# Recurrent mixer's diagonal in its last level, value transposition after the decay transposition, masks ahead of the scores, compression input evicted in one piece

## What is computed

```python
# compression: segments of 16 tokens, 31 overlapping blocks of 32
flat = blocks.transpose(0, 1, 3, 2, 4).reshape(B, ncmp, G, CMP_LEN * dh)
return jax.nn.gelu(flat @ w1) @ w2
...
# recurrence, inside a chunk of 64 tokens: every pair s <= t, with its decay
decay = jnp.exp(jnp.where(causal[:, :, None], b[:, :, :, None, :] - b[:, :, None, :, :], -jnp.inf))
attn = jnp.einsum('bhtd,bhsd,bhtsd->bhts', qc, kc, decay)
...
# attention: scores of a query block, masked
s = jnp.einsum('bhmqd,bhmkd->bhmqk', qblk, kh).astype(jnp.float32) * scale
p = jax.nn.softmax(jnp.where(allowed, s, neg), axis=-1)
```

## Time and profile before

| | |
|---|---|
| three runs | 1952.78, 1953.26, 1955.55 us |
| median | 1953.26 us |
| the profiled execution, its own time | 1954.02 us |
| its span in the trace | 1952.2 us |
| mean granted clock of TensorE in it | 0.999 |
| PE busy | 98% of the span |
| VectorE, ScalarE, GpSimd busy | 47%, 43%, 45% |

### The profile page before, as it was taken

How to read it: one execution, slowest core, us unless ns; L and a number is a source line. 1 busy time by engine, 2 the same in 40 slices (tenths; PEclk the granted TensorE clock), 3 DMA queues, 4 the chain that set the end, 5 groups by cost and what they waited for, 6 DMA issues and landing times. The chain is left out here.

```text
span 1952.2 us, 25554 instructions
## 1 busy us (share of the span) xinstructions
PE 1919.8 (98%) x9142; PEld 1506.3 (77%) x9142; DVE 915.8 (47%) x1423; ACT 834.1 (43%) x1269; POOL 881.5 (45%) x1185
## 2 busy tenths in 40 slices
PE   8999999999999999999999999999999999999998
PEld 7766666888888887777688888887777688888887
DVE  6587877432231346777541313233777643222132
ACT  4456565543342355555532223134555543222233
POOL 4322211556456465343456456454443255454553
PEclk9999999999999999999999999999999999999999
DMA  8211111233233233222133233333222233243322
GB/s 229 65 44 44 33 44 33 87 108 108 87 91 115 77 96 98 76 66 76 55 104 113 81 104 100 85 98 96 76 67 75 65 87 110 85 119 86 109 86 76
DMA packets 318099, 168.50 MB, mean 86 GB/s; under 512 B 15027, under 2 KB 313494, under 8 KB 317846
## 3 DMA queue, kind: packets, MB, share of 16 engines
q1 hardware_dynamic: 314432, 162.38, 29.0%
q10 hardware_dynamic: 3542, 4.50, 0.9%
HBM read 160.29 MB, written 2.10 MB: 83 GB/s over the span
## 5 line engine op out<-in xcount | busy, mean ns | idle before, releaser
L744 POOL TENSOR_TENSOR wlo<-raw,whi 128x256 fp32r<-128x256 f32 x1160 | 864.4, 778 | 1039.5 <-ACT whi L791 1039.5
L1641 PE MATMUL accs<-Xh,whi 128*128 128x512 f32 x1448 | 581.2, 401 | 1.8 <-POOL wlo L744 1.8
L1642 PE MATMUL accs<-Xl,whi 128*128 128x512 f32 x1448 | 563.9, 389 | 0.0
L1644 PE MATMUL accs<-Xh,wlo 128*128 128x512 f32 x1440 | 562.0, 390 | 0.0
L791 ACT ACTIVATE whi<-raw 128x1024 fp32r<-128x1024 f32 x291 | 307.7, 1061 | 267.1 <-PE accs L1644 218.7
L1641 PEld LDWEIGHTS accs<-Xh,whi 128*128 128x128 f32 x1448 | 272.0, 188 | 60.1 <-POOL wlo L744 3.9
L1642 PEld LDWEIGHTS accs<-Xl,whi 128*128 128x128 f32 x1448 | 272.3, 188 | 56.3 <-issue 3.6
L1644 PEld LDWEIGHTS accs<-Xh,wlo 128*128 128x128 f32 x1440 | 270.3, 188 | 58.2
L1641 PE MATMUL accs<-Uh,whi 128*128 128x512 f32 x744 | 289.7, 389 | 0.8 <-DVE xT L1222 0.8
L1642 PE MATMUL accs<-Ul,whi 128*128 128x512 f32 x744 | 289.5, 389 | 0.0
L1644 PE MATMUL accs<-Uh,wlo 128*128 128x512 f32 x744 | 289.4, 389 | 0.0
(11 more groups left out here) (305 smaller groups left out, 1910.9 us busy)
## 6 DMA issues: line engine op xcount, KB each, us to landing
raw<-in_w_ff_dram SPq DMA_DIRECT2D x128, 512.0 KB
raw<-in_w_in_dram SPq DMA_DIRECT2D x71, 512.0 KB
raw<-in_w_gate_up_dram SPq DMA_DIRECT2D x44, 512.0 KB
raw<-in_w_down_dram SPq DMA_DIRECT2D x16, 512.0 KB
raw<-in_w_o_dram SPq DMA_DIRECT2D x16, 512.0 KB
px<-W ACTq DMA_DIRECT2D x64, 64.0 KB, 2.0
raw<-in_w_down_dram SPq DMA_DIRECT2D x8, 384.0 KB
W<-in_x_dram SPq DMA_DIRECT2D x4, 512.0 KB, 6.1
```

The lines of the kernel that those rows point to most:

```text
L744: pool.tensor_tensor(lo[:, ks], raw[:, unit_no % RAW, ks], hi[:, ks].bitcast(F32), ALU.subtract).then_inc(sems["wlo"], 1)
L1641: mmul(y, whi[:, slot, k], xh[:, k], start=(i == 0), stop=False)
L1642: last = mmul(y, whi[:, slot, k], xl[:, k], start=False, stop=("both" in u and i == len(ks) - 1))
L1644: last = mmul(y, wlo[:, slot, k], xh[:, k], start=False, stop=(i == len(ks) - 1))
```

## The change

It has five parts.

1. `hd` is gone. The mask of the last level has ones on its diagonal too. In that level (`m == 1`) the decays are made for 256 elements instead of 512, VectorE multiplies the odd key positions by exp(-d) and the odd query positions by exp(d) in place, in two instructions of 256 elements each, and PE multiplies keys and queries themselves: on the diagonal the factors cancel. `hP` of level 0 initialises `HA` by a product with its mask.
2. In `ORDER`, `vt2` comes behind `cb` and `ha2` for heads 0 to 2. In `LAST1` only `hd` is dropped.
3. In `n1`, `s1` and `d1` the mask matmuls come first and open the sum; the scores are added to them.
4. In `n1`, `s1` and `d1` the wait for the query or key (`nq_ok`, `sbk_ok`, `rope_ok`) stands behind the masks.
5. `evc` takes the unit out in one product of 128x512 into `q4`, which frees the bank. Two VectorE copies and two new ScalarE copies (64x256 each, strided) then make what the four products made.

```diff
+    lev[:, -1] += np.eye(P)
...
-    ("mmA", 0, "hg"), ("vt", 0), ("hd", 0), ("vt2", 0, "hv"), ("cb", 0), ("ha2", 0), ("n1", 0, 0, 2), ("mmB", 0, "hg"), ("hD", 0, 0),
+    ("mmA", 0, "hg"), ("vt", 0), ("cb", 0), ("ha2", 0), ("vt2", 0, "hv"), ("n1", 0, 0, 2), ("mmB", 0, "hg"), ("hD", 0, 0),
...
# ScalarE, evc
+                    act.wait_ge(sems["acc"], at("acc", 1))
+                    for g, odd in ((0, 1), (1, 0)):
+                        r = hrows(g)
+                        A(kcx[n][r].rearrange("p (h s) -> p h s", s=32), every2(t[r], odd), ACT.Copy).then_inc(sems["cmp_t" if g else "act"], 1)
# VectorE, evc
-                    for g, odd in ((0, 1), (1, 0)):
-                        r = hrows(g)
-                        TTn(kcx[n][r].rearrange("p (h s) -> p h s", s=32), every2(y[r], odd), every2(rstd[r], odd), ALU.mult).then_inc(sems["cmp_t" if g else "dve"], 1)
+                    t = q4[:, 3 - n]
+                    scaled(t, 1 - n)
                     for g, odd in ((0, 0), (1, 1)):
-                        TTn(kc2[n][r, g].rearrange("p (h s) -> p h s", s=32), every2(y[r], odd), every2(rstd[r], odd), ALU.mult).then_inc(sems["acc" if g else "dve"], 1)
+                        CP(kc2[n][r, g].rearrange("p (h s) -> p h s", s=32), every2(t[r], odd)).then_inc(sems["cmp_e" if g else "dve"], 1)
# VectorE, hd (removed) and hF of the last level
-                    TTn(HA, TT[:, 0, :].rearrange("p (b n) -> p b n", n=P), ident.unsqueeze(1).to_broadcast([P, NB, P]), ALU.mult).then_inc(sems["T_dve"], 1)
+                    if m == 1:
+                        k1, q1 = odds(hk[i % 2]), odds(hq[i % 2])
+                        TTn(k1, k1, HD[:, a % 2, T // 2:T], ALU.mult).then_inc(sems["dve"], 1)
+                        dve.wait_ge(sems["dve"], chained())
+                        TTn(q1, q1, HD[:, a % 2, 0:T // 2], ALU.mult).then_inc(sems["hl_f"], 1)
# VectorE, hP
+                    if a == 0:
+                        TTn(HA, F2, mask.bitcast(F32).unsqueeze(1).to_broadcast([P, NB, P]), ALU.mult).then_inc(sems["T_dve"], 1)
# PE, hd (removed)
-                    for b in range(NB):
-                        r = slice(P * b, P * b + P)
-                        last = mmul(TT[:, 0, r], hk[p][:, r], hq[p][:, r], start=True, stop=True)
# PE, n1 (s1 and d1 in the same way)
-                    pe.wait_ge(sems["nq_ok"], at(f"q{i}"))
                     pe.wait_ge(sems["S_act"], at("S_act"))
                     pe.wait_ge(sems["S_dve"], at("S_dve"))
                     for g in range(2):
-                        mmul(S[:, g, 0:n], q4[hrows(g), i % 2, P * qb:n], kts[a][hrows(g), 0:n], start=True, stop=False)
+                        mmul(S[:, g, n - P:n], identb, m_causal, start=True, stop=False, skip_group_check=True)
+                    pe.wait_ge(sems["nq_ok"], at(f"q{i}"))
                     for g in range(2):
-                        last = mmul(S[:, g, n - P:n], identb, m_causal, start=False, stop=True)
+                        last = mmul(S[:, g, 0:n], q4[hrows(g), i % 2, P * qb:n], kts[a][hrows(g), 0:n], start=False, stop=True, skip_group_check=True)
```

More of the change, by code:

```diff
@@ L101 @@
     "resid": dict(acc=1),
-    "evc": dict(acc=1, cmp_t=1),
+    "evc": dict(acc=1, cmp_t=1, cmp_e=1),
     "cmp1": dict(M_fill=1, M_dve=1, g_in=1, g_e=1, g_ok=1),
@@ L160, in marks_of @@
         return dict(xt_ok="acc")
-    if kind == "evc":
-        return {f"evc{item[1]}": "acc"}
     if kind == "mixo":
@@ L631, in hrows, with odds @@
             return slice(64 * g, 64 * g + 64)
+        def odds(v):
+            return v.rearrange("p (n t) -> p t n", t=2)[:, 1]
         def every2(v, odd):
@@ L1436, in stage @@
                     dve.wait_ge(sems["T_fill"], at(f"hF{a}"))
-                    dve.copy_predicated(HA, mask.unsqueeze(1).to_broadcast([P, NB, P]),
-                                            TT[:, a % 2, :].rearrange("p (b n) -> p b n", n=P)).then_inc(sems["T_dve"], 1)
+                    F2 = TT[:, a % 2, :].rearrange("p (b n) -> p b n", n=P)
+                    if a == 0:
+                        TTn(HA, F2, mask.bitcast(F32).unsqueeze(1).to_broadcast([P, NB, P]), ALU.mult).then_inc(sems["T_dve"], 1)
+                    else:
+                        dve.copy_predicated(HA, mask.unsqueeze(1).to_broadcast([P, NB, P]), F2).then_inc(sems["T_dve"], 1)
                     dve.wait_ge(sems["T_dve"], at("T_dve", 1))
@@ L1684, in stage @@
                     n = item[1]
-                    pe.wait_ge(sems["acc"], at(f"evc{n}"))
+                    pe.wait_ge(sems["cmp_e"], n + 1)
                     pe.wait_ge(sems["M_act"], at("M_act"))
@@ L1794, in stage @@
                     last.then_inc(sems["T_fill"], 1)
[L1795 to L1801, removed]
-                    for b in range(NB):
-                        r = slice(P * b, P * b + P)
-                        last = mmul(TT[:, 0, r], hk[p][:, r], hq[p][:, r], start=True, stop=True)
-                    last.then_inc(sems["T_fill"], 1)
                 elif kind == "hF":
@@ L1809, in stage @@
                     pe.wait_ge(sems["T_dve"], at(f"T{a % 2}_free"))
-                    F = HD[:, a % 2]
+                    p, F = item[1] % 2, HD[:, a % 2]
+                    ks, qs = (hk[p], hq[p]) if LEVELS[a] == 1 else (F, F)
                     for b in range(NB):
                         r = slice(P * b, P * b + P)
-                        last = mmul(TT[:, a % 2, r], F[:, r], F[:, r], start=True, stop=True)
+                        last = mmul(TT[:, a % 2, r], ks[:, r], qs[:, r], start=True, stop=True)
                     last.then_inc(sems["T_fill"], 1)
@@ L1843, in stage @@
                     for h in range(2):
-                        mmul(S[:, h, 0:n], sbq[hrows(h), P * qb:n], sbk[hrows(h), 0:n], start=True, stop=False)
+                        mmul(S[:, h, n - P:n], identb, m_sb, start=True, stop=False, skip_group_check=True)
+                    pe.wait_ge(sems["acc"], at("sbk_ok"))
                     for h in range(2):
-                        last = mmul(S[:, h, n - P:n], identb, m_sb, start=False, stop=True)
+                        last = mmul(S[:, h, 0:n], sbq[hrows(h), P * qb:n], sbk[hrows(h), 0:n], start=False, stop=True, skip_group_check=True)
                     last.then_inc(sems["S_fill"], 1)
@@ L1873, in stage @@
                     for m in range(2):
-                        mmul(TT[:, m, 0:n], dfq[hrows(m), P * qb:n], dfk[hrows(m), 0:n], start=True, stop=False)
+                        mmul(TT[:, m, n - P:n], identb, m_chunk, start=True, stop=False, skip_group_check=True)
+                    pe.wait_ge(sems["rp"], at("rope_ok"))
                     for m in range(2):
-                        last = mmul(TT[:, m, n - P:n], identb, m_chunk, start=False, stop=True)
+                        last = mmul(TT[:, m, 0:n], dfq[hrows(m), P * qb:n], dfk[hrows(m), 0:n], start=False, stop=True, skip_group_check=True)
                     last.then_inc(sems["T_fill"], 1)
```

37 lines of the change are left out of this document (19 added, 18 removed).

## The result

| | before | after |
|---|---|---|
| median of 8 runs | 1954.61 us | 1961.35 us |
| lowest, highest | 1952.78, 1956.91 | 1957.98, 1962.90 |
| ratio of the times | | 1.0031, 95% interval 1.0023 to 1.0040 |
| span of the profiled execution | 1952.2 | 1958.1 |
| mean granted clock of TensorE in it | 0.999 | 0.997 |

The change is slower by 0.31%, which is 6.1 us; the two medians lie 6.7 apart. 1961.35 lies inside the stated range (1952.5 to 1961.5), just under its upper end; the forecast was 1957.0. The ratio asks for 6.1 where the sum had 3.8. Further down, one execution of the kernel with parts 3 to 5 took 2127.32 us at a mean clock of 0.851 and is left out of that kernel's ratio.

A forecast was written before the change was run, and what follows sets the result against it. The prediction took TensorE, busy 98% of the span, as the bound. Terms -1.55 + 0 + 3.6 + 1.8 + 0.45 - 0.5 = +3.8 us gave 1957.8 for a profiled execution, median 1957.0; range 1952.5 to 1961.5.

The forecast's parts named there:

- The eviction, -1.55: Head of the program: one product frees the bank, so PE's unit at 28.42 starts earlier; -1.55 us, ends -1.0 and -1.74.
- The limit that I set: Head of the program: VectorE free about 1.4 earlier, plus 0.18 in hand on PE, caps the gain near 1.55 us.
- `hd`'s removal, 0: Between the halves of `hg`: `hd`'s 3.6 us on PE lies beside a wait, `cb` stays at 96.82; gain 0.
- rival C: PE's idle pieces around `cb` and `vt2` drop the clock to 1.2 GHz, up to +2.7 us per head; about 1963, chance 0.06.
- `vt2`, +3.6: Heads 0 to 2: moved behind `ha2`, it waits for VectorE's copy out of `M`; +1.25, +1.16, +1.16, together +3.6 us.
- Masks first, +1.8: The 96 score items: raw sum +4.0 us, less what waits swallow and stretches priced elsewhere, leaves +1.8; ends -0.8 and +4.0.
- Two prices: Per score item with masks first: +0.05 us between large matmuls, -0.09 ahead of a 64-wide tile.
- the third: Per score item with masks first where PE was waiting before it: +0.14 us, for 22 items.
- Rival E: Score items: only changes of tiling mode count, -0.75 us net instead of +1.8; 1954.5, chance 0.17.
- Rival B: Score items: the masks cost their raw sum, +4.0 us instead of +1.8, as earlier results swallow nothing; about 1960.5, chance 0.13.
- The last level +0.45: VectorE's two products of 256 instead of one of 512 delay `hF` on PE in heads 0 to 2: 3 x 0.15 us.
- head 3 -0.5: Head 3: the `hd` product of 0.69 leaves VectorE's queue, -0.33 us, and scores ready earlier give twice 0.09.

The follow-up runs named there:

- the kernel with parts 3 to 5: The kernel before with masks first and the eviction in one piece, `hd` kept and `vt2` at its old place: median 1951.04 us, ratio 0.9982.
- with part 1: The changed kernel with `vt2` put back at its old place ahead of `cb` in heads 0 to 2: 1952.99 us, ratio 0.9993 to the kernel before.
- filler: The changed kernel with `hd`'s four matmuls put back on PE, result unused, VectorE's product still away: 1955.85 us, ratio 1.0005 to the kernel before.
- the masks alone: The kernel before with only the hunks of `n1`, `s1` and `d1` (masks open the sums): 1952.53 us, ratio 0.9988.
- doubled filling: The changed kernel with twice as many unused `hd` matmuls put back on PE (loop over `NB * 2`): 1958.37 us, ratio 1.0017 to the kernel before.

## Why the prediction was right in sign and short in size

Traces with like falls give the work of each part. There are two readings, and they differ by the steps behind 928, where executions of one program differ too. The first goes by PE's place at 928 against the kernel before, with the scatter ahead of 27 taken off: parts 3 to 5 -1.7, with part 1 -0.3, with part 2 and `hd`'s matmuls kept +3.3, the changed kernel +7.1. So -1.7, +1.4, +3.6, and +3.9 for the clock. The second goes by whole spans without a fall ahead of the last microseconds: before 1951.9 and 1952.2, parts 3 to 5 1949.2, with part 1 1950.1, with `hd`'s matmuls kept 1953.9, and the changed kernel 1958.1 with its two falls: -2.7, +0.9, +3.8, and +4.2. Work is thus +2.0 to +3.3, and the clock about +4 in this trace.

**The eviction, -1.55: right in its wait, and near in number by two errors that cancel.** The releaser was `evc`, and all of the 1.74 arrived. The limit that I set, VectorE's lateness at the next unit, came out wrong. At the end of the second `evc` VectorE was only 0.7 earlier (4.28 us of work instead of 4.95), where the sum had 1.6, as three of the four copies took 0.71 to 0.82. With 0.18 in hand that would have given PE 0.85. But at the next unit VectorE was 2.8 earlier (32.24 instead of 35.04 of the earlier trace rows), 0.4 of which was there at the start. The difference is small instructions of the parameter step behind the `evc`s, which were slow before, and they were no term of the sum. VectorE's row before, with GpSimd's beside it, and VectorE's in the profile after:

```profile
31.91 0.79 POOL L744 TENSOR_TENSOR wlo<-raw,whi 128x256 fp32r<-128x256 f32 x1 [2.82 <-ACT whi L791]
32.14 1.28 DVE L1156 TENSOR_TENSOR small<-vec 64x2 f32<-64x2 f32 x2
```

```profile
31.08 0.35 DVE L1166 TENSOR_TENSOR small<-vec 64x2 f32<-64x2 f32 x2
```

No run was made for it, but the traces tell what they ran beside. Before, GpSimd makes four parts of `wlo` from 31.91 to 34.79, and the four small products in that time take 0.47 to 0.67 each; a fifth, at 34.84, takes 0.17. After, GpSimd has nothing to do between 29.04 and 32.87, and all five take 0.16 to 0.17. The six traces without part 5 agree with the first and the eight with it with the second. ScalarE's copies cost nothing, as said, though they took 0.65 to 0.68 and not 0.42.

**`hd`'s removal, 0: right for the queue, wrong for the time.** `cb` came where it had been, 2.79 behind the start of the last large matmul (2.91 before). But "hidden by a wait" was taken as worthless. Those 1.0 us of matmuls split PE's idle time, and with `vt2` moved behind, their absence cost about 5 us of median. The step that failed is this zero, together with rival C: it was priced and given 0.06, because it was to be decided by the length of the idle piece alone. The earlier trace rows show 1.84 idle with no fall behind it, and I read that as a sign of safety. One execution's trace can't show that: in another one of the same program the clock fell exactly there. And length alone doesn't decide: the 2.40 of head 0 is the longest of them and had no fall in either profile.

**`vt2`, +3.6: right.** Against the kernel that differs in the place of `vt2` (and has no filler), the steps at the three heads are 1.19, 1.18 and 1.20, for 1.25, 1.16 and 1.16. Against the kernel before they are 1.18, 1.35 and 1.36, with what part 1 costs in heads 1 and 2; alone, 1.28 to 1.32 a head. The gap ahead of it was 1.22, for 1.4.

**Masks first, +1.8: wrong, between 0 and -0.6 in the traces (1951.6 against 1951.9 and 1952.2, and within 0.1 at 928).** Two prices were right (+0.05, -0.09), and the third was 0.10 for 0.14. What failed is the sum of them. I had 22 items pay behind a wait, and 13 did; and an item that is 0.05 longer shows only if nothing behind it waits, and I let ten items be absorbed where nearly all were. Rival E, -0.75, was nearer, though its reason (only mode changes count) is refuted by the +0.05. Rival B, the raw sum of +4.0, is out, although its 1960.5 is the price that came nearest to 1961.35.

**The last level +0.45 and head 3 -0.5: near, with one step missed.** The products took 2 x 0.43 for the 2 x 0.42 assumed. Part 1 shows as +0.6 ahead of head 3 (0.45 of it at 279 in one pair of traces) and gives back 0.25 there, so about +0.35 against the -0.05 of the sum. The rest of its +1.4 is the scan at 777, which no term had: what starts earlier or later on GpSimd was not asked.

So the forecast of +3.8 was made of a work sum that should have been +2.0 to +3.3, and it lacked +4 of clock. That the range held the result is luck in part: two errors of opposite sign, and a range whose upper end was drawn to take in B, which is refuted, and to leave out C, whose mechanism it was. The largest error among the work terms is the masks (1.8 to 2.4 too high); against it stand part 1 with the scan (1.0 to 1.5 too low), and the rest is within what two executions differ by.

**Open.** Why the masks alone ran at 0.999 or 1.000 in all eleven runs, when the kernel before beside it was at 0.998 or less in 19 of 33 (the expectations say 20), with the same gap at 28.4; why that share was 15 of 33 and 2 of 15 in the other two sets, which ran on other chips; and why doubled filling did worse than single. Why an idle piece brings the clock down in one execution and not in another, and why head 0 was spared, wasn't tried. That the filler works by keeping PE busy is shown in so far as it moved nothing else: `cb`, `ha2` and `vt2` start where they did relative to the last large matmul. How much work in a gap is right is not shown.

## What to carry to other kernels

Before taking "free" matmuls out of a wait of TensorE, add up the idle time around it: if the next instruction of TensorE waits again soon, work without use in the first gap can be worth more than the time it takes. Time it, as twice as much of it did worse here. Move a transposition only after asking which copy frees its bank; here two users of one bank side by side cost 1.2 us per head, as the second stood behind two copies of VectorE of 0.69 each. Ask of every engine that starts at another time what it will now run beside. And take several executions of the kernel before, with their clocks, before calling any gap harmless: here the spread of its own runs (1953 to 1957 us) was the clock, and was as large as the forecast.

## What the runs showed of the hardware

- The granted clock fell to 0.50 behind idle pieces of 0.7 to 2.2 us, some of them with a second piece a microsecond or two behind the first; a fall cost 1.6 us at 28, 1.6 at 931, 1.4 in head 3, 2.4 in head 1 in one profile, and in the other 1.1 there and 2.4 in head 2. It came in some executions only and in different heads of one program, and never in head 0, whose idle piece of 2.40 was the longest.
- Some VectorE instructions are slower when GpSimd is at work on `wlo` as they begin: a small product of two SBUF operands took 0.47 to 0.67 us instead of 0.15 to 0.17, a copy of 64x256 with a stride 0.68 to 0.90 instead of 0.38 or 0.39, a scan of 128x512 1.57 to 1.79 instead of 1.22 or 1.23. A scan that began ahead of GpSimd's work kept its 1.22, though GpSimd worked beside the rest of it.
- A bf16 mask of 128x128 ahead of the scores costs little more or less than behind them: 0.05 more between large matmuls, 0.09 less ahead of 64-wide tiles.
